# Two norms of a transformer block taken one sequence at a time between float32 GEMMs split in two parts, with the next stage's first weight tiles kept aside

## What is computed

```
x   = x   + g1  * y_lat           # y = mixer output @ ev_w_out
x   = x   + g2  * conv_ffn(modulate(rms_norm(x,   norm2_g[0]), sh2,  sc2),  ...)
ctx = ctx + g1c * y_ctx
ctx = ctx + g2c * conv_ffn(modulate(rms_norm(ctx, norm2_g[0]), sh2c, sc2c), ...)
# the second layer begins with its own norms of both:
h_lat = modulate(rms_norm(x,   norm1_g[1]), sh1,  sc1)
h_ctx = modulate(rms_norm(ctx, norm1_g[1]), sh1c, sc1c)
```

## Time and profile before

| | |
|---|---|
| runs shown | 2519.22, 2514.03, 2519.58 us; median 2519.22 |
| the profiled execution | 2514.51 us, span 2512.8 us |
| PE busy | 2436.4 us, 97% of the span |
| DVE busy | 1761.3 us, 70% |
| ACT busy | 1175.8 us, 47% |
| mean granted TensorE clock | 0.986 of full speed |

### The profile page before, as it was taken

The page is one execution under the profiler, slowest core; times in us unless marked ns, Lnnn a source line. Parts: engine busy times, 40 slices in busy tenths (PEclk is TensorE's granted clock), DMA queues, the critical chain, the costliest instruction groups (busy, mean ns, idle before and its releaser), DMA issues.

```text
span 2512.8 us, 47344 instructions
## 1 busy us (share of the span) xinstructions
PE 2436.4 (97%) x17988; PEld 2231.9 (89%) x17988; DVE 1761.3 (70%) x2854; ACT 1175.8 (47%) x1817; POOL 108.6 (4%) x161
## 2 busy tenths in 40 slices
PE   8999999999999999989999999999989999989998
PEld 6866777778798999988999998999989999978998
DVE  5879799988756875775765767665567657676665
ACT  4554422233545444555544544544545446465444
POOL 1211000000000000000400000000000000000000
PEclk9999999999999999999999999999999999999999
DMA  7323255555433555421455531555415554321554
GB/s 300 143 101 133 94 192 180 191 174 169 157 105 127 192 183 169 135 93 60 168 185 180 171 126 68 173 182 189 151 59 172 187 178 151 110 93 68 201 178 132
DMA packets 119706, 378.17 MB, mean 150 GB/s; under 512 B 11655, under 2 KB 29063, under 8 KB 119184
## 3 DMA queue, kind: packets, MB, share of 16 engines
q1 hardware_dynamic: 107040, 328.62, 38.7%
q0 software_dynamic: 12528, 47.62, 5.5%
HBM read 375.15 MB, written 1.05 MB: 150 GB/s over the span
## 4 chain that ended last, share of the span: by engine, by line
PE 86%; DVE 7%; ACT 4%; issue 2%; DMA 1%; SPq 0%; DVEq 0%; ACTq 0%
PE gb L633 23%; PE gb L634 22%; PE gb L635 22%; PE mb L712 2%; PE mb L2734 2%; DVE w_lo L602 1%; ACT w_hi L594 1%; PE gb L2715 1%; PE mb L634 1%; PE mb L633 1%; PE mb L635 1%; DVE W L2469 1%; DMA Pj<-in_mod 1%; PE gb L684 1%; PE gb L686 1%
## 5 line engine op out<-in xcount | busy, mean ns | idle before, releaser
L633 PE MATMUL gb<-Xs,w_hi 128*128 128x256 f32 (+1 forms) x3456 | 1063.7, 308 | 18.3 <-DVE w_lo L602 5.0
L635 PE MATMUL gb<-Xs,w_lo 128*128 128x256 f32 (+1 forms) x3456 | 1047.2, 303 | 0.0
L634 PE MATMUL gb<-Xs,w_hi 128*128 128x256 f32 (+1 forms) x3376 | 1016.9, 301 | 0.0
L594 ACT ACTIVATE w_hi<-raw 128x1024 fp32r<-128x1024 f32 x592 | 620.8, 1057 | 744.6 <-PE gb L635 689.5
L602 DVE TENSOR_TENSOR w_lo<-raw,w_hi 128x1024 fp32r<-128x1024 f32 x592 | 720.8, 1229 | 218.4 <-ACT w_hi L594 211.6
L633 PEld LDWEIGHTS gb<-Xs,w_hi 128*128 128x128 f32 x3456 | 655.0, 190 | 72.5 <-issue 28.2
L635 PEld LDWEIGHTS gb<-Xs,w_lo 128*128 128x128 f32 x3456 | 654.8, 189 | 30.9
L634 PEld LDWEIGHTS gb<-Xs,w_hi 128*128 128x128 f32 x3376 | 640.2, 190 | 27.3 <-issue 2.2
L634 PE MATMUL gb<-Fs,w_hi 128*128 128x256 f32 (+1 forms) x960 | 278.3, 290 | 0.0
L633 PE MATMUL gb<-Fs,w_hi 128*128 128x256 f32 (+1 forms) x880 | 247.4, 281 | 0.0
L635 PE MATMUL gb<-Fs,w_lo 128*128 128x256 f32 (+1 forms) x880 | 246.4, 280 | 0.0
(11 more groups left out here) (428 smaller groups left out, 3150.0 us busy)
## 6 DMA issues: line engine op xcount, KB each, us to landing
raw<-in_up SPq DMA_DIRECT2D x264, 512.0 KB, 3.2
raw<-in_down SPq DMA_DIRECT2D x96, 512.0 KB, 3.7
R<-in_mod_later POOLq DMA_DIRECT2D x80, 512.0 KB, 3.8
raw<-in_gdn_in SPq DMA_DIRECT2D x64, 512.0 KB, 3.2
raw<-in_down SPq DMA_DIRECT2D x48, 384.0 KB, 3.9
raw<-in_hgrn_in SPq DMA_DIRECT2D x32, 512.0 KB, 4.2
raw<-in_ev_in SPq DMA_DIRECT2D x24, 512.0 KB, 5.4
raw<-in_gla_in SPq DMA_DIRECT2D x24, 512.0 KB, 4.0
```

What stands on the lines that cost most here:

```text
L594: nc.scalar.activation(hi, raw[:, slot, 0:hi.shape[1]] if len(hi.shape) == 3 else pairs(raw[:, slot]), ACT.Identity).then_inc(*hi_ready.inc())
L633: nc.tensor.matmul(to, weight_block(w_slot, 0, k), x_hi, start=start, stop=False)
L634: nc.tensor.matmul(to, weight_block(w_slot, 0, k), x_lo, start=False, stop=False)
L635: return nc.tensor.matmul(to, weight_block(w_slot, 1, k), x_hi, start=False, stop=stop)
```

## The change

In the first layer both norms go sequence by sequence.

- In ev_out and in the rest of down0, PE computes tiles 0 to 3 as before, then tiles 4 to 7 for the first 256 columns (half_out), then tiles 4 to 7 for the second 256 columns. DVE adds the first halves to X, and the first sequence's squares are summed by PE in the middle of tile 4's second pass (pe_seq_stats(pe, 0)).
- Its norm then runs row by row on DVE and ACT with 256 columns (dve_seq_norm and act_seq_norm, called in place of act_squares, act_rms, dve_residual and dve_rms), while PE is in the second pass. Residuals, squares and sums of the second sequence are put between the rows, at the row numbers in EV_BESIDE and DOWN0_BESIDE.
- PE begins the next stage with the first sequence of its three tiles (pe_seq_group), puts the second sequence's sum of squares after row 1, and does the second sequence after all rows of the first. pe_warm is gone after both norms.
- ACT writes the high part to Xs directly from the scaled row (no copy on DVE); rows with an even number are scaled twice by ACT, odd ones by DVE's tensor_scalar.
- Since the four slots stay in use by tiles 4 to 7, the next stage's tiles 0, 1 and 2 are split into rows 2 to 13 of Fs (FIRST_ASIDE).
- In down0 the sums of the first 16 hidden rows for tiles 4 to 7 are closed and added to X by DVE on their own (8 more instructions, wide_taken), and the rest of those tiles starts new sums, the second sequence in the banks mb 0 to 2 and gb 3 (rest_bank).

```
+        FIRST_ASIDE = SLOTS + 5
+        aside_of.update({first_of[name] + u: FIRST_ASIDE + u for name in ("up0", "od_in") if name in first_of for u in range(AHEAD)})
...
+        SEQ = (slice(0, T), slice(T, 2 * T))
+        BY_SEQ = range(4, KC)
+        EV_BESIDE = {4: 0, 5: 2, 6: 4, 7: KC}
+        DOWN0_BESIDE = {4: 0, 5: 1, 6: 2, 7: 3}
+
+        def pe_seq_stats(pe, s):
+
+            pe.wait_ge(*sums_kept.due("pe"))
+            nc.tensor.matmul(sbank[:, SEQ[s]], ones[:, :], sq_sum(2 * T)[:, SEQ[s]], start=True, stop=False)
+            pe.wait_ge(*sq_ready.due("pe", 4 if s else 8))
+            nc.tensor.matmul(sbank[:, SEQ[s]], ones[:, :], squares_at(KC - 1, 2 * T)[:, SEQ[s]], start=False, stop=True).then_inc(*sum_done.inc())
+
+        def pe_seq_group(pe, tiles, s, stats_at=None, last=()):
+
+            for k in range(KC):
+                pe.wait_ge(*h_ready.due("pe"))
+                for u in tiles:
+                    done = pe_block(gb[:, u, SEQ[s]], FIRST_ASIDE + u if u < AHEAD else u, k, Xs[:, k, SEQ[s]], Xs[:, KC + k, SEQ[s]], k == 0, k == KC - 1)
+                    if k == KC - 1 and u in last:
+                        done.then_inc(*gemm_out.inc())
+                if k == stats_at:
+                    pe_seq_stats(pe, 1)
...
+            if by_seq:
+                for u in range(AHEAD):
+                    pe.wait_ge(*lo_ready.due("pe"))
+                    pe.wait_ge(*gemm_taken.free("pe"))
+                pe_seq_group(pe, range(AHEAD), 0, stats_at=1)
+                pe_seq_group(pe, range(AHEAD), 1, last=range(AHEAD))
...
+        def pe_out_by_seq(pe, ready, order):
+
+            pe_group(pe, 0, 2 * T, ready, order)
+            for m in range(AHEAD, KC):
+                pe.wait_ge(*lo_ready.due("pe"))
+                pe.wait_ge(*gemm_taken.free("pe"))
+                cols = SEQ[0] if m in BY_SEQ else slice(0, 2 * T)
+                for k in range(KC):
+                    last = pe_block(gb[:, m % BANKS, cols], m % SLOTS, k, Xs[:, k, cols], Xs[:, KC + k, cols], k == 0, k == KC - 1)
+                last.then_inc(*(half_out if m in BY_SEQ else gemm_out).inc())
+            for m in BY_SEQ:
+                pe.wait_ge(*half_taken.due("pe"))
+                for k in range(KC):
+                    last = pe_block(gb[:, m % BANKS, SEQ[1]], m % SLOTS, k, Xs[:, k, SEQ[1]], Xs[:, KC + k, SEQ[1]], k == 0, k == KC - 1)
+                    if m == BY_SEQ[0] and k == 3:
+                        pe_seq_stats(pe, 0)
+                last.then_inc(*gemm_out.inc())
...
+        def rest_bank(m, s):
+
+            return (mb[:, m - 4, :] if m < KC - 1 else gb[:, 3, :]) if s and m in BY_SEQ else down_banks[m]
...
@@ -758,17 +819,27 @@
                 for m in range(KC):
                     if k == 0 and m in (4, 6):
                         pe.wait_ge(*gemm_taken.seen("pe", 6 - m))
-                    last = pe_block(down_banks[m], k % SLOTS, m, hidden_hi(k), Fs[:, k, :], k == 0, False)
+                    last = pe_block(down_banks[m], k % SLOTS, m, hidden_hi(k), Fs[:, k, :], k == 0, k == WIDE - 1 and m in BY_SEQ)
                 last.then_inc(*gemm_out.inc())
             pe.wait_ge(*hidden_ready.due("pe", FC - 1 - HIDDEN_ORDER.index(WIDE - 1)))
             for m in range(KC):
                 pe.wait_ge(*lo_ready.due("pe"))
+                cols = SEQ[0] if m in BY_SEQ else slice(0, 2 * T)
+                if m == BY_SEQ[0]:
+                    pe.wait_ge(*wide_taken.due("pe"))
                 for k in range(WIDE, FC):
-                    last = pe_block(down_banks[m], m % SLOTS, k - WIDE, hidden_hi(k), Fs[:, k, :], False, k == FC - 1)
+                    last = pe_block(rest_bank(m, 0)[:, cols], m % SLOTS, k - WIDE, hidden_hi(k)[:, cols], Fs[:, k, cols],
+                                    k == WIDE and m in BY_SEQ, k == FC - 1)
+                last.then_inc(*(half_out if m in BY_SEQ else gemm_out).inc())
+            gemm_taken.free("pe", KC)
+            pe.wait_ge(*gemm_taken.seen("pe", 5))
+            for m in BY_SEQ:
+                pe.wait_ge(*half_taken.due("pe"))
+                for k in range(WIDE, FC):
+                    last = pe_block(rest_bank(m, 1)[:, SEQ[1]], m % SLOTS, k - WIDE, hidden_hi(k)[:, SEQ[1]], Fs[:, k, SEQ[1]], k == WIDE, k == FC - 1)
+                    if m == BY_SEQ[0] and k == WIDE + 3:
+                        pe_seq_stats(pe, 0)
                 last.then_inc(*gemm_out.inc())
-            gemm_taken.free("pe", KC)
-            pe_stats(pe, 2 * T, False)
-            pe_warm(pe, 8)
...
+        def act_seq_norm(act, layer, norm, beside_row):
+
+            use_table(LN_EXP)
+            for m in range(BY_SEQ[0]):
+                act_tile(act)
+                act.wait_ge(*gemm_taken.due("act"))
+                if m > 2:
+                    act.wait_ge(*sq_added.due("act"))
+                nc.scalar.activation(squares_at(m, 2 * T) if m else sq_sum(2 * T), X[:, m, :], ACT.Square, scale=1 / 32).then_inc(*sq_ready.inc())
+
+            def square(m, s):
+                if s:
+                    act.wait_ge(*gemm_taken.due("act"))
+                    if m > BY_SEQ[1]:
+                        act.wait_ge(*sq_added.due("act", 2 if m == BY_SEQ[2] else 1))
+                else:
+                    act.wait_ge(*half_taken.due("act"))
+                    act.wait_ge(*sq_added.due("act"))
+                nc.scalar.activation(squares_at(m, 2 * T)[:, SEQ[s]], X[:, m, SEQ[s]], ACT.Square, scale=1 / 32).then_inc(*sq_ready.inc())
+
+            def root(s):
+                act.wait_ge(*sum_done.due("act_sum"))
+                alink(act, nc.scalar.activation(W[:, 2, SEQ[s]], sbank[:, SEQ[s]], ACT.Ln, bias=eps[:, 0:1]))
+                nc.scalar.activation(W[:, 3, SEQ[s]], W[:, 2, SEQ[s]], ACT.Exp, scale=-0.5).then_inc(*rstd_ready.inc())
+
+            def shifted(m, s):
+                act.wait_ge(*normed.due("act"))
+                t = W[:, 4 + m % 4, SEQ[s]]
+                affine_of = dict(bias=modv[:, layer, 24 * norm + m, s:s + 1], scale=modA[:, layer, norm, m, s:s + 1])
+                last = nc.scalar.activation(Xs[:, m, SEQ[s]], t, ACT.Identity, **affine_of)
+                if m % 2 == 0:
+                    last = nc.scalar.activation(t, t, ACT.Identity, **affine_of)
+                last.then_inc(*affine.inc())
+
+            act.wait_ge(*gemm_out.seen("act"))
+            for m in BY_SEQ:
+                if m < KC - 1:
+                    act_tile(act)
+                square(m, 0)
+            root(0)
+            act.wait_ge(*mod_ready.due("act"))
+            for k in range(KC):
+                shifted(k, 0)
+                for m in BY_SEQ:
+                    if beside_row[m] == k or (beside_row[m] == KC and k == KC - 1):
+                        square(m, 1)
+                        if m == KC - 1:
+                            act_tile(act)
+            root(1)
+            for m in range(KC):
+                shifted(m, 1)
+            sq_added.due("act")
...
+        def dve_seq_norm(dve, part, layer, norm, mods_done, beside_row, beside=None, banks=None):
+
+            def residual(m, s):
+                bank = banks(m, s) if banks else gb[:, m % BANKS, :]
+                return nc.vector.scalar_tensor_tensor(out=X[:, m, SEQ[s]], in0=bank[:, SEQ[s]], scalar=modv[:, 0, part * KC + m, s:s + 1],
+                                                      in1=X[:, m, SEQ[s]], op0=ALU.mult, op1=ALU.add)
+
+            def sums(m, s):
+                dve.wait_ge(*sq_ready.due("dve"))
+                dve.wait_ge(*sq_added.sent())
+                nc.vector.tensor_tensor(sq_sum(2 * T)[:, SEQ[s]], sq_sum(2 * T)[:, SEQ[s]], squares_at(m, 2 * T)[:, SEQ[s]],
+                                        ALU.add).then_inc(*sq_added.inc())
+                if m == KC - 2:
+                    dve.wait_ge(*sq_added.sent())
+                    nc.vector.memset(small[:, 156:157], 0.0).then_inc(*sums_kept.inc())
+
+            def taken(m):
+                dve.wait_ge(*gemm_out.due("dve"))
+                gemm_taken.due("dve")
+                residual(m, 1).then_inc(*gemm_taken.inc())
+
+            def scaled(m, s):
+                if m >= 4:
+                    dve.wait_ge(*h_ready.sent())
+                nc.vector.tensor_tensor(W[:, 4 + m % 4, SEQ[s]], X[:, m, SEQ[s]], W[:, 3, SEQ[s]], ALU.mult).then_inc(*normed.inc())
+
+            def low(m, s):
+                t = W[:, 4 + m % 4, SEQ[s]]
+                dve.wait_ge(*affine.due("dve"))
+                if m % 2:
+                    link(dve, nc.vector.tensor_scalar(t, t, modA[:, layer, norm, m, s:s + 1], modv[:, layer, 24 * norm + m, s:s + 1], ALU.mult, ALU.add))
+                nc.vector.tensor_tensor(Xs[:, KC + m, SEQ[s]], t, Xs[:, m, SEQ[s]], ALU.subtract).then_inc(*h_ready.inc())
+
+            if banks:
+                dve.wait_ge(*gemm_out.seen("dve"))
+                for m in BY_SEQ:
+                    residual(m, 0).then_inc(*dve_step.inc())
```

(65 more changed lines are left out.)

43 lines of the change are left out of this document (22 added, 21 removed).

## The result

| | before | after |
|---|---|---|
| median of 20 runs | 2517.64 us | 2508.72 us |
| lowest to highest | 2509.4 to 2520.96 | 2505.48 to 2514.41 |
| ratio of after to before, 95% interval | | 0.9966, 0.996 to 0.9972 |
| span of the profiled execution | 2512.8 us | 2504.5 us |

The change makes the kernel 0.34% faster, 8.6 us of 2517.64 by the ratio (7.0 to 10.1 by its interval).

What follows compares the result with a forecast made beforehand. PE, busy 97% of the span, was taken as the bound, with 14.95 us lost at two norms. Gains of 4.1 (first norm) and 3.7 (second) sum to 7.8: 2519.2 to 2511.4 us, range 2504.5 to 2516.5.

Steps and rivals of the forecast that it cites:

- The ceiling and PE's work: Both norms cost PE 14.95 us, the most to gain; cutting 288 matmuls into 576 on 256 columns costs nothing.
- Rival 4: Slower: 256-column matmuls cost over half of 512-column ones with weights in Fs or two streams meeting; 2520.9 or more; chance 0.05.
- The first sum: In ev_out's second pass PE waits for DVE and ACT at the first sequence's sum: new wait of 2.06 us.
- The rows and the second sum: First norm: rows stay ahead of PE, no wait at the second sum; up0's three tiles end 4.85 us earlier.
- What up0 leaves: DVE sets up0's pace and starts when tile 0 is out: 4.85 less 0.7 leaves 4.1 us.
- The second norm: After down0: partial-sum residuals hidden, wait of 0.25 us at the first sum, four od_in tiles end 7.65 us earlier.
- What od_in leaves: PE waits 1.65, 0.4 and 1.4 us in od_in behind ACT's and DVE's queued work; 3.7 us is left.
- Rival 1: Waits shorter than counted, DVE starts its loop with PE, ACT's copies in time: gain 10.5, 2508.7 us; chance 0.22.
- Rival 2: Waits longer, 1 us more at each norm and each of the two next stages: gain about 4, 2515.2 us; chance 0.25.
- Rival 3: Clock falls after the 2.06 us wait at the first sum, losing 1.7 us: gain 6.1, 2513.1 us; chance 0.04.
- Rival 5: PE stands at up0's start because rows aren't ready, if tile 7's last residual precedes them; inside the longer-waits chance of 0.25.
- The level: Starting time from which the gain was subtracted: median of the runs shown, 2519.2 us.

Runs made afterwards that it cites:

- n1_only: Kernel after with its second half undone (norm after down0 and start of od_in as in the kernel before); ratio to before 0.9997.
- tail_by_tile: Kernel after, with PE doing the last four rows of the second sequence in up0's first group tile by tile; ratio to before 0.9965.
- sum_earlier: Kernel after with PE's first sum over partitions three blocks earlier; ran once, 2512.39 us, no ratio.
- before_nowarm: Kernel before without the 15 useless matmuls after its two norms in the first layer; ratio to before 1.0008.
- before_aside: Kernel before with only the first three weight tiles of up0 and od_in split into rows 2 to 13 of Fs; ratio to before 1.0008.
- keeps_first: Kernel after with ACT's copies of od_in's tiles 0 and 1 before its decay tables, DVE's first two rotary steps before combining them; ratio to before 0.9954.
- aside_apart: Kernel after with the tiles in Fs laid out as high parts in rows 2 to 7, low parts in 8 to 13; ran once, 2513.94 us.

## Why the prediction was right, and where it wasn't

Times of the kernel after are set back by 0.48 us here where they stand against the prediction's (A was later by that).

- **The ceiling and PE's work.** Nothing for the cut was right for weights in w_hi and w_lo, where 256 columns go at 0.117. With three tiles in Fs they go at 0.120: 144 matmuls by 0.003, some 0.45 us that the sum lacked. Rival 4 had the place (weights in Fs) and not the size: its d was 0.014 to 0.03.
- **The first sum.** Predicted: PE ready for it at 272.5, DVE's flag at 274.05, PE on with its blocks at 275.45. In n1_only (A earlier by 0.31): 272.63, 273.92 and 275.23. Against 0.86 us for the sums, PE lost 1.74 us, not 2.06: it came 0.13 later, the flag 0.13 earlier, and the rest is less than 0.1.
- **The rows and the second sum.** PE's second pass was to end at 285.25; it did at 285.22 in after (285.70 less 0.48). No wait at up0's start nor at the second sum, right. The group was to end at 302.9 and did at 303.34: the 0.45 of the pace.
- **What up0 leaves.** 4.85 less 0.7 was to be 4.1; it was 4.41 less 0.69, 3.72. The step that lost 0.7 was right in kind and size: tail_by_tile gets it back and more.
- **The second norm.** The eight residuals of the partial sums end at 633.5 in after, ten us before PE needs them: hidden, as counted. The first sum there: L671 to L673 takes 0.61 us for 0.43, a wait of 0.18, predicted 0.25. Four tiles of od_in end 7.44 us earlier counted from B (376.16 for 383.60), predicted 7.65.
- **What od_in leaves.** Waits of 1.65, 0.4 and 1.4 were predicted. The last doesn't follow from its own times: turns that end at 691.2 where 688.5 + 0.86 = 689.4 was possible are 1.8 late, and 3.9 in all is what the 3.7 left of 7.65 is worked out with. The profile's brackets have 1.25, 0.23 and 1.07 (0.42 and 0.65), but they count from modelled ends, and they leave out that the matmuls behind a wait start slower: after the turn at 681.12 the next tile begins 1.37 later, 0.67 in before, and 0.23 of that is its wait. Counted from start to start, against the same steps in before, the three places cost 1.40, 0.62 and 1.55 us, 3.57 in all. So 7.44 less 3.57 leaves 3.87 us (tile 5 starts 384.06 us behind B, before 387.93), where 3.7 were forecast. The path was right; the first and last place were 0.25 and 0.3 too dear, the second 0.2 too cheap.
- **The rivals.** Rival 1 named 2508.7, which is the median found, but not by its mechanism: its shorter waits would have shown as 10.5 us at C, and there are 7.58. Rival 2 is excluded by the same mark. Rival 3: the granted clock is 1.00 from 274 to 277, from 285 to 303 and from 653 to 680 in after, and stays 1.00 behind the waits of 1.24 us (n1_only) and 1.00 (sum_earlier). A new wait of 2.06 us never arose; the longest has 1.25. Rival 5: PE doesn't stand at up0's start.
- **The clock.** It wasn't lost where I looked and was lost where I hadn't. Eight of twelve profiles show 1.2 GHz behind the wait of 2.97 us near 237, four don't, with the same work around it. The Trainium skill, "TensorE: Matmul & The Clock Gate", "Part 1: The HAM clock gate", says that the number of slow matmuls varies from run to run with the same kernel. The traces agree as far as they can, since each is of another kernel with the same code at this place: none, or 7 to 14 of them. What it states of the throttled state as the default fits before_nowarm, where a gap of 4.63 us was followed by 0.50.
- **The reason given against rival 3 was weak.** The earlier trace rows has the clock up to the end of the wait of 1.97 us, not behind it. Behind it the clock of before did stay at 1.00 (786.3 to 789.0), but behind the same wait before_aside had 0.62 (788.1 to 790.8). Behind a wait of 2.00 us near 199, which all twelve profiles have, the clock fell to 1.2 GHz in seven: 0.50 in after (197.4 to 200.0), 1.00 in before (199.4 to 202.0). So a wait of 2 us is not one that does no harm, and a chance of 0.04 for rival 3 was too low.
- **The level.** I put the gain on the median of three runs, which was 1.6 us high. That is more than the sum was off: 0.2 us by the marks, 0.8 by the ratio.

## What to carry to other kernels

A gap of one engine between stages can be closed by doing the boundary in halves, but what remains of it is set by who is next: here half of 15 us is gained, since the first sum waited for DVE, up0 starts only when DVE has a whole tile, and od_in's turns stood behind ACT's tables in a fixed order. After such a change look for queued work that was hidden behind the old gap and move it, as keeps_first did for 2.5 us. Where stages untouched vary by several us, count a change between two marks that both traces share, not by the spans, and see whether the clock was the same between the marks.

## What was not expected of the hardware

- One wait of 2.97 us is followed by 1.2 GHz in eight of twelve executions, for 7 or 8 matmuls on 512 columns in five of them (after: 8, 1.6 us lost) and for 13 or 14 in three (aside_apart: some 5.5 us long, 2.7 lost). A wait of 2.00 us is followed by it in seven of twelve, the waits of 1.0 to 1.25 us at the sums and turns in none. Stretches behind C, the same code in all, took 1806.1 to 1816.3 us.
- Matmuls whose weights all lie in Fs start every 0.120 us on 256 columns and every 0.227 on 512; with weights in w_hi and w_lo it is 0.117 and 0.233. Where blocks of a tile in Fs alternate with those of one in w_hi (od_in's second sequence), it is 0.117. The layout inside Fs doesn't matter (aside_apart).
- Useless matmuls between two stages kept the clock at 2.4 GHz (granted 1.00 from 284 to 294 in before) and held the next stage up by 1.2 and 2.1 us; without them the clock fell to 0.50, and the time was the same within 0.2%.
